# Three small buffers placed in front of the split weights: every weight tile starts 448 bytes further on

## What is computed

```python
proj = h @ w_in[l]                                  # 1024 x 3080
x = x + o @ w_out[l]                                # 1024 x 1024
u = causal_dwconv(h @ w_up[l], conv_w[l], conv_b[l])  # 1024 x 5632
x = x + (jax.nn.silu(gate) * val) @ w_down[l]       # 2816 x 1024
...
qkv = (h @ w_qkv)                                   # 1024 x 3072
b_gate, c_gate, u = jnp.split(h @ w_in, 3, axis=-1) # 1024 x 3072
g, u = jnp.split(h @ w_gate_up, 2, axis=-1)         # 1024 x 5632, in both layers
return (jax.nn.silu(g) * u) @ w_down                # 2816 x 1024, in both layers
```

## Time and profile before

| | us |
|---|---|
| median of three runs | 911.48 |
| profiled execution, its time | 911.66 |
| profiled execution, its span from first to last instruction | 909.7 |
| TensorE busy (matmuls) | 900.3 |
| VectorE busy | 749.3 |
| ScalarE busy | 503.3 |
| GpSimd busy | 49.5 |

### The profile page before, as it was taken

How to read it: one execution, slowest core, us unless ns; L and a number is a source line. 1 busy time by engine, 2 the same in 40 slices (tenths; PEclk the granted TensorE clock), 3 DMA queues, 4 the chain that set the end, 5 groups by cost and what they waited for, 6 DMA issues and landing times.

```text
span 909.7 us, 18262 instructions
## 1 busy us (share of the span) xinstructions
PE 900.3 (99%) x7367; PEld 875.8 (96%) x7367; DVE 749.3 (82%) x1032; ACT 503.3 (55%) x776; POOL 49.5 (5%) x87
## 2 busy tenths in 40 slices
PE   8999999999999999999999999999999999999998
PEld 7999999999999989999999999999999999999886
DVE  6999989999899789898987887987998887667544
ACT  6446757666665467764754444436645564444531
POOL 5100000000001000010000100100000000000000
PEclk9999999999999999999999999999999999999999
DMA  9887375666667947575469988984687467664541
GB/s 288 281 282 270 115 244 197 220 222 207 231 232 278 325 137 255 169 268 192 139 205 325 335 301 314 328 268 149 199 280 260 139 229 251 235 213 180 186 139 47
DMA packets 132129, 207.71 MB, mean 228 GB/s; under 512 B 4711, under 2 KB 109537, under 8 KB 126945
## 3 DMA queue, kind: packets, MB, share of 16 engines
q1 hardware_dynamic: 123968, 156.47, 51.3%
q0 software_dynamic: 8064, 50.34, 15.9%
q10 hardware_dynamic: 32, 0.01, 0.0%
HBM read 205.75 MB, written 1.05 MB: 227 GB/s over the span
## 4 chain that ended last, share of the span: by engine, by line
PE 91%; DVE 5%; ACT 2%; issue 1%; DMA 1%; SPq 0%; ACTq 0%; DVEq 0%
PE bank L1673 25%; PE bank L1675 25%; PE bank L1674 25%; PE bank L1828 2%; PE bank L1744 2%; PE bank L1753 2%; PE bank L1742 2%; PE bank L1710 1%; PE bank L1718 1%; PE bank L1712 1%; DVE w_lo L1002 1%; DMA w_raw<-in_w_in 1%; ACT w_hi L582 1%; PE bank L2028 0%; PE bank L2157 0%
## 5 line engine op out<-in xcount | busy, mean ns | idle before, releaser
L1002 DVE TENSOR_TENSOR w_lo<-w_raw,w_hi 128x1024 fp32r<-128x1024 f32 x294 | 353.8, 1221 | 107.6 <-ACT w_hi L582 105.4
L582 ACT ACTIVATE w_hi<-w_raw 128x1024 fp32r<-128x1024 f32 x293 | 306.1, 1056 | 242.3 <-PE bank L1675 226.7
L1673 PE MATMUL bank<-act_hi,w_hi 128*128 128x256 f32 x1312 | 366.1, 279 | 0.1
L1675 PE MATMUL bank<-act_hi,w_lo 128*128 128x256 f32 x1312 | 363.0, 277 | 0.0
L1674 PE MATMUL bank<-act_lo,w_hi 128*128 128x256 f32 x1312 | 363.0, 277 | 0.0
L1673 PEld LDWEIGHTS bank<-act_hi,w_hi 128*128 128x128 f32 x1312 | 246.5, 188 | 0.7 <-issue 0.6
L1674 PEld LDWEIGHTS bank<-act_lo,w_hi 128*128 128x128 f32 x1312 | 246.6, 188 | 0.4 <-issue 0.2
L1675 PEld LDWEIGHTS bank<-act_hi,w_lo 128*128 128x128 f32 x1312 | 246.6, 188 | 0.0
L1018 DVE SCALAR_TENSOR_TENSOR ada_acc<-ada_raw,silu_c,ada_acc 128x2048 f32<-128x2048 f32 (+1 forms) x56 | 114.3, 2040 | 1.7 <-DMA ada_raw<-in_w_ada 1.4
L1673 PE MATMUL bank<-hid_hi,w_hi 128*128 128x256 f32 x352 | 98.2, 279 | 0.0
L1674 PE MATMUL bank<-hid_lo,w_hi 128*128 128x256 f32 x352 | 97.2, 276 | 0.0
(11 more groups left out here) (309 smaller groups left out, 1374.0 us busy)
## 6 DMA issues: line engine op xcount, KB each, us to landing
w_raw<-in_w_gate_up SPq DMA_DIRECT2D x44, 1024.0 KB, 5.2
ada_raw<-in_w_ada POOLq DMA_DIRECT2D x40, 1024.0 KB, 5.3
w_raw<-in_w_down SPq DMA_DIRECT2D x33, 1024.0 KB, 5.1
w_raw<-in_w_in SPq DMA_DIRECT2D x23, 1024.0 KB, 6.8
w_raw<-in_w_up SPq DMA_DIRECT2D x22, 1024.0 KB, 5.7
w_raw<-in_w_qkv SPq DMA_DIRECT2D x12, 1024.0 KB, 7.3
w_raw<-in_w_out SPq DMA_DIRECT2D x8, 1024.0 KB, 7.0
ada_raw<-in_w_ada POOLq DMA_DIRECT2D x16, 512.0 KB, 4.9
```

Source lines behind the costliest of these rows:

```text
L582: act.activation(unit(w_hi, u), raw_half(c, h), ACT.Copy).then_inc(hi_ready, 1)
L1002: dve.tensor_tensor(unit(w_lo, u), raw_half(c, h), unit(w_hi, u).bitcast(F32), ALU.subtract).then_inc(lo_ready, 1)
L1673: pe.matmul(dst, a_hi, b_hi, start=start, stop=False, skip_group_check=True)
L1675: return pe.matmul(dst, a_lo, b_hi, start=False, stop=stop, skip_group_check=True)
```

## The change

The three declarations of `mod`, `silu_c` and `silu_e` move from behind `res` to a place between `w_raw` and `w_hi`. Nothing else is edited: the instructions, their order, their shapes and their semaphores stay as they are, and the sum of all sizes stays the same.

```diff
         w_raw = sb("w_raw", [P, RAW, 2 * UNIT])
+        mod = sb("mod", [P, 2, 6 * KT])
+        silu_c = sb("silu_c", [P, KT])
+        silu_e = sb("silu_e", [P, KT])
         w_hi = sb("w_hi", [P, SPLIT, UNIT], F32R)
         w_lo = sb("w_lo", [P, SPLIT, UNIT], F32R)
         res = sb("res", [P, KT, T])
-        mod = sb("mod", [P, 2, 6 * KT])
-        silu_c = sb("silu_c", [P, KT])
-        silu_e = sb("silu_e", [P, KT])
         act_hi = sb("act_hi", [P, KT, T], F32R)
         act_lo = sb("act_lo", [P, KT, T], F32R)
```

## The result

The changed kernel takes 945.44 us (median of four runs, 945.04 to 945.84) against 911.56 (median of four of the kernel before, 911.25 to 913.55); the ratio is 1.0371 (95% interval 1.0359 to 1.0383). That is 33.9 us slower. The profiled execution has a span of 943.8 us, 34.1 more than before.

What follows compares the result with a forecast made beforehand. TensorE was taken to bound the kernel: number of matmuls times their start-to-start distance, plus some gaps. Every part was taken as 0, so 911.66 + 0 for the profiled execution, 911.5 us for the median; range 893 to 918.

Steps and rivals of the forecast that it cites:

- The small buffers, `res` and the splits: Column reads of mod, silu_c, silu_e, readers of res, and the ScalarE and VectorE weight splits: new addresses cost 0.
- TensorE's operands: Matmul operands at new offsets, the only place with leverage: taken as 0, bounds +19.1 us loss and -37 us gain.
- the exchanged roles: Weights moving at 128 with activations standing at 64 show the same 113.5 and 117.6 ns, so placement gives 0.
- The third reason: If moving stream and weight load met in memory, loss should grow with loads; 512 columns lose 15.5 ns, 256 lose 11.1.
- The second reason: TensorE weight loads take 188 ns in either role, so the operands' place does not matter.
- The remark on loads alone at 113 ns: Eight weight loads beside one-column products come at 113 ns, so 113.3 may be the rate of loading alone.
- Slower: Rival, chance 0.19: the long stretches take the slow rhythm, 917.8 us for the first alone, 930.6 for all six.
- the long stretches: Six unbroken TensorE stretches of products, 481.0 us in all, at 113.3 ns; +19.1 us if all ran at 117.8.
- the slow pieces: 23 TensorE pieces in the attention stages at 117.8 ns, 87.07 us in all; at most 3.3 us back at 113.3.
- The bound from the 258-column runs: All the long stretches at the 121 ns of 258-column products: +33 us, set aside for their two extra columns.
- Its other half: TensorE's rhythm is decided where a run begins behind a wait, then kept; a slow first feed-forward stretch costs 6.3 us.
- Faster: Rival, chance 0.28: part of the excess over 109 ns comes from operand offsets; equal ones give 908.2 to 874.5 us.

Runs made afterwards that it cites:

- v5: v1 with 192 bytes more of small buffers (rinv, x_rms) in front of ident, so the constants return to offset 352: 912.73 us, ratio 1.0002.
- the scans: Kernels of their own running series of 48 products, with operand offsets, columns, format and beginnings varied; float32r with 256 columns took 113.3 to about 120 ns a product.
- v2: Kernel before the change with q_rstd (64 bytes) in front of act_hi, moving act from 64 to 128 while the weights stay at 128: 937.2 us.
- v3: Changed kernel with 448 bytes of small buffers between res and act_hi, putting act at 0 with the weights at 64: 919.94 us.
- v1: Changed kernel's order with small buffers added so large operands keep the offsets of before; constants went from 352 to 160: 921.82 us, ratio 1.0095.
- v6: Kernel before the change with rowsum, nmax and f_cum in front of ident, moving constants from 352 to 160, large operands unmoved: 923.34 us, ratio 1.0107.

## Why the prediction was wrong

**What bounds the kernel: right.** TensorE's distance between products, times their number, is the time; ScalarE and VectorE wait 41 and 30 us longer and work as long as before, to within 2 us.

**The small buffers, `res` and the splits: right.** `mod` in front of `w_hi` costs nothing in v5 (ratio 1.0002), the splits stay at 1055 and 1221 ns, and the readers of `res` at 476 ns (line 1133) and 493 ns (line 613), its transposes at 272 ns.

**TensorE's operands: wrong, 0 for +34 us.** The step that failed is the first of the three rows, the exchanged roles. I read the earlier trace rows as "either operand may lie at 64 or at 128". They show differences of 64 and -64 (192 modulo 256) and no other; the difference 0, which is what the change makes everywhere, is in no row. The prediction said so in one place and took 0 all the same. Nor do they tell these two apart: both values, 113.3 and 117.8, stand in either role, and the scans find both for 64 and for 192. What the runs showed in place of the 0 is a third rhythm, 120.0 ns, for the difference 0. v2 and v3 show it in the kernel: same places, other differences, and the loss follows the difference.

The third reason failed too. It said that a loss by the meeting of two streams must grow with the number of loads, and that a shift of the start can't remove a meeting. In the scan 512 columns range from 227 to 234 ns by the difference, with one load each, and with 256 columns even a load of 32 leaves a range of 113.3 to 120.0. From "the loss does not grow with the loads" it does not follow that the offset is without effect. The second reason, loads of 188 ns in either role, was no evidence: after the change they show as 192, 4 ns for a distance that grew by 6.7.

The remark on loads alone at 113 ns did not hold either: with loads of 64 and of 32 columns, whose records are shorter (134 and 108 ns against 189), the fastest series still runs at 113.3.

**The skill's rule.** By the independent ports of the Trainium skill (page "TensorE: Matmul & The Clock Gate", section "Step-by-step: what each phase is for") no offset could matter. For bfloat16 and float32 the runs agree with it, 109.1 and 216 ns at all differences; for float32r they do not, and the measurement decides. The estimate from the formula of its section "Back-to-back issue gap", 109.2 ns for 256 columns (the page calls it the isolated gap), is met by bfloat16 here (109.1) and by no float32r series (113.3 at best).

**The rivals.** "Slower" had the right sign and place: the long stretches leave the 113.3 ns. Its price was the mis-sized term: it took the slow rhythm that the trace showed, 117.8 ns and +19.1 us, while equal offsets have a rhythm of their own, 120.0 ns, which also takes in the slow pieces. The bound from the 258-column runs, 121 ns and +33 us, stood in the text and was put aside because those runs have two columns more; 911.5 + 33 = 944.5 would have been 1 us from the result, by luck: the long stretches cost 28.3, and the rest came from products that this bound leaves out. Its other half, that one start decides for a whole stretch, came true where I had not looked for it, in v1 and v6: the execution of v1 whose first feed-forward part ran slow took 928.21 us against the 921.8 of the others, near the 6.3 computed. "Faster" is refuted: equal offsets give 120.0 ns, and no float32r series of 256 columns in the scans goes under 113.3.

**The range** ended at 918, at one long stretch in the slow rhythm. For an operand case that no row shows, it should have ended at the highest distance that any full-rate row shows.

## What to carry to other kernels

Where TensorE streams float32r with 128 stationary and 256 moving columns, place the operands so that their SBUF addresses differ by 64 modulo 256 (stationary minus moving): it gave 113.3 ns from most starts and 117.8 from the others, while equal offsets always gave 120.0, 6% over the best. For other shapes measure a few differences first; with 64 stationary columns and with 512 moving ones equal offsets were the best. Change the order of buffers only with their offsets written beside them: a move of a few hundred bytes shifts everything behind it, and the profile shows it only as another distance between matmuls. When a row is to show that something does not matter, write down the variable that it holds fixed; an exchange of two operands holds the size of their difference fixed.

## What the runs showed of the hardware

The distance between float32r products of 128 x 128 by 256 depends on the difference of the two SBUF offsets: in this kernel it is 113.3, 117.8 or 120.0 ns, in the scan it repeats when the stationary operand moves by 256 bytes. bfloat16 (109.1 ns) and plain float32 (216 ns for a record) show no dependence. A stream keeps its rhythm over 1396 products and across the turns of a loop. Which one it takes is set at its start: by five columns more of a float32 product in front (the only one of seven such shifts that did it), by the places of the float32 constants and small buffers (911.7 against 923.3 us), and for some stretches by something that changes between executions of one kernel: two groups of times 2 us apart, or one run 6.4 us above the others. Why offsets matter at all, which of the small buffers sets a start, why 258 columns are indifferent (121 ns before and after), and why 512 moving or 64 stationary columns prefer the difference 0 stays open.
